# Forgetting attention's output projection: weight units in alternating order, more steps inside the last heads

## The reference, cut to what matters

```python
q, k, v, f_logit = jnp.split(x @ w_in, [D, 2 * D, 3 * D], axis=-1)
c = cumsum(log_sigmoid(f_logit + b_f))
s = q @ k.T * HEAD_DIM ** -0.5 + c[t] - c[s]     # per head, causal
o = softmax(s) @ v
return o @ w_o                                   # 1024 x 1024
```

## Time and profile before

| | us |
|---|---|
| median of three runs | 1881.05 |
| the profiled execution | 1880.14 |
| its span, first to last instruction | 1878.3 |
| PE busy | 1858.2 |
| DVE busy | 926.3 |
| ACT busy | 706.8 |

### The profile page before, as it was taken

The page is one execution under the profiler, slowest core; times in us unless marked ns, Lnnn a source line. Parts: engine busy times, 40 slices in busy tenths (PEclk is TensorE's granted clock), DMA queues, the critical chain, the costliest instruction groups (busy, mean ns, idle before and its releaser), DMA issues.

```text
span 1878.3 us, 24126 instructions
## 1 busy us (share of the span) xinstructions
PE 1858.2 (99%) x8779; PEld 1529.3 (81%) x8779; DVE 926.3 (49%) x1336; ACT 706.8 (38%) x1162; POOL 24.4 (1%) x44
## 2 busy tenths in 40 slices
PE   9999999999998999999999999999999999999998
PEld 7888888877776888888888888888888788888888
DVE  5444434356886544444344444434379644444332
ACT  5232223246775432323233232323267432322332
POOL 1000000000000000000000000000000000000000
PEclk9999999999999999999999999999999999999999
DMA  5223223331111332332333223223323223232332
GB/s 169 94 97 100 88 91 103 121 96 64 55 57 34 102 101 90 100 98 81 102 111 112 91 99 100 87 88 107 121 82 82 82 90 100 89 100 89 93 104 85
DMA packets 56521, 176.33 MB, mean 94 GB/s; under 512 B 6800, under 2 KB 9360, under 8 KB 56464
## 3 DMA queue, kind: packets, MB, share of 16 engines
q1 hardware_dynamic: 56320, 175.54, 29.3%
q10 hardware_dynamic: 144, 0.03, 0.0%
HBM read 171.48 MB, written 2.10 MB: 92 GB/s over the span
## 4 chain that ended last, share of the span: by engine, by line
PE 95%; DVE 2%; ACT 1%; issue 0%; DMA 0%; POOL 0%; DVEq 0%; SPq 0%; POOLq 0%; ACTq 0%
PE bank L454 91%; PE bank L800 1%; PE bank L812 1%; PE bank L910 0%; ACT scratch L1345 0%; DVE w_lo L1418 0%; ACT wide_hi L1295 0%; PE bank L480 0%; PE bank L517 0%; PE bank L523 0%; PE bank L514 0%; DVE wide_lo L1832 0%; DVE wmax L1816 0%; DMA scratch<-x_dram 0%; DVE wide_lo L1824 0%
## 5 line engine op out<-in xcount | busy, mean ns | idle before, releaser
L1418 DVE TENSOR_TENSOR w_lo<-raw,w_hi 128x1024 fp32r<-128x1024 f32 (+1 forms) x343 | 392.4, 1144 | 816.9 <-ACT w_hi L1017 815.6
L1017 ACT ACTIVATE w_hi<-raw 128x1024 fp32r<-128x1024 f32 (+1 forms) x343 | 341.3, 995 | 846.3 <-PE bank L454 843.9
L454 PE MATMUL bank<-u_hi,w_hi 128*128 128x512 f32 (+1 forms) x1592 | 630.2, 396 | 0.3 <-DVE w_lo L1418 0.3
L454 PE MATMUL bank<-u_hi,w_lo 128*128 128x512 f32 (+1 forms) x1592 | 620.2, 390 | 0.0
L454 PE MATMUL bank<-u_lo,w_hi 128*128 128x512 f32 (+1 forms) x1592 | 620.0, 389 | 0.0
L454 PEld LDWEIGHTS bank<-u_hi,w_lo 128*128 128x128 f32 (+1 forms) x1592 | 298.1, 187 | 63.6
L454 PEld LDWEIGHTS bank<-u_hi,w_hi 128*128 128x128 f32 (+1 forms) x1592 | 298.6, 188 | 61.0 <-issue 1.1
L454 PEld LDWEIGHTS bank<-u_lo,w_hi 128*128 128x128 f32 (+1 forms) x1592 | 298.6, 188 | 59.4 <-issue 1.0
L454 PE MATMUL bank<-wide_hi,w_hi 128*128 128x512 f32 (+1 forms) x816 | 316.1, 387 | 0.8 <-issue 0.5
L454 PE MATMUL bank<-wide_hi,w_lo 128*128 128x512 f32 (+1 forms) x816 | 314.7, 386 | 0.0
L454 PE MATMUL bank<-wide_lo,w_hi 128*128 128x512 f32 (+1 forms) x816 | 314.6, 386 | 0.0
(11 more groups left out here) (186 smaller groups left out, 1279.6 us busy)
## 6 DMA issues: line engine op xcount, KB each, us to landing
raw<-ffn_in_dram SPq DMA_DIRECT2D x175, 512.0 KB, 3.2
raw<-ffn_out_dram SPq DMA_DIRECT2D x128, 384.0 KB, 3.0
raw<-mix_w_dram SPq DMA_DIRECT2D x51, 512.0 KB, 3.3
y_dram<-raw SPq DMA_DIRECT2D x8, 256.0 KB, 2.7
wide_hi<-wide_hi SPq DMA_DIRECT2D x7, 256.0 KB, 2.8
scratch<-x_dram SPq DMA_DIRECT2D x2, 512.0 KB, 8.0
raw<-ffn_in_dram SPq DMA_DIRECT2D x2, 256.0 KB, 3.7
scratch<-x_dram SPq DMA_DIRECT2D x2, 256.0 KB, 4.0
```

Of the source, the lines that this page charges most:

```text
L454: mm = pe.matmul(out, a, b, start=first and k == 0, stop=last and k == n - 1)
L1017: act.activation(w_hi[:, slot, 0:cols], raw[:, (base + r) % RAW, 0:cols], ACT.Copy)\
L1418: dve.tensor_tensor(w_lo[:, s, 0:cols], raw[:, r, 0:cols], f32(w_hi[:, s, 0:cols]), ALU.subtract).then_inc(w_ready, 1)
```

## The change

The eight output units lie in memory in the order `WO_ORDER`, as pairs (m, k): the first four alternate between pair 0 and pair 1. Unit 26 is thus (1, 0) and unit 27 is (0, 1). The host puts the weights in that order. `fox_out_pairs` replaces `first_out_pairs` for this mixer (the sliding window keeps the old one): seven steps of pair 0 (units 25 and 27), then seven of pair 1 (26 and 28), then kb 7 of each. The first output step moves to the sixth filler place of t = 13, and t = 16 uses four places. On ACT and DVE the step that splits unit 27 moves from the end of t = 15 to the end of t = 14, and the two pairs' residuals come after the third and the fourth unit instead of the second and the fourth.

```diff
+WO_ORDER = ((0, 0), (1, 0), (0, 1), (1, 1), (2, 0), (2, 1), (3, 0), (3, 1))
...
-            def out_pair(n, m, ready, per_pair):
+            def out_pair(n, m, ready, per_pair, unit_of=lambda m, k: len(WO_KBS) * m + k):
...
-                    at = n + len(WO_KBS) * m + k
+                    at = n + unit_of(m, k)
...
+            def interleaved(m, k):
+                return WO_ORDER.index((m, k))
+
+            def fox_out_pairs(n):
+                pairs = [out_pair(n, m, o_ready, 2, interleaved) for m in range(2)]
+                pe.wait_ge(qk_scaled, 2 * PAIRS)
+                for _ in range(PAIRS - 1):
+                    next(pairs[0])
+                    yield
+                pe.wait_ge(expd, TB * HEADS)
+                for _ in range(PAIRS - 1):
+                    next(pairs[1])
+                    yield
+                for pair in pairs:
+                    for _ in pair:
+                        pass
...
-                    yield from first_out_pairs(n + 2 * PAIRS - 2, [0] * 7 + [1], (qk_scaled, 2 * PAIRS), o_ready, 2,
-                                               (expd, TB * HEADS))
+                    yield from fox_out_pairs(n + 2 * PAIRS - 2)
...
-                    allowed = {HEADS - 3: range(KB - AHEAD), HEADS - 2: (0, 3, 6), HEADS - 1: (0, 3, 6),
-                               HEADS: (0, 4)}.get(t, range(KB))
+                    allowed = {HEADS - 3: range(KB - AHEAD + 1), HEADS - 2: (0, 3, 6), HEADS - 1: (0, 3, 6),
+                               HEADS: (3, 4, 5, 6)}.get(t, range(KB))
...
-                        if r % len(kbs) == len(kbs) - 1:
-                            post_pair(nn, 4 * i, 2 * (r // len(kbs)))
+                        done = ends if ends is not None and type(i) is int and i == 0 else pair_ends
+                        if r in done:
+                            post_pair(nn, 4 * i, 2 * done.index(r))
...
-                    if j + 1 < PAIRS or t == HEADS - 1:
+                    if j + 1 < PAIRS or t == HEADS - 2:
                         step(n)
                         n += 1
-                out_stage(n - 1, nn + 1, WO_KBS, UNIT, first_split=True)
+                out_stage(n - 1, nn + 1, WO_KBS, UNIT, first_split=True, ends=(2, 3))
...
-    mix_w = np.concatenate([w_v[0:1], w_f, w_v[1:5], qk[0:2], w_v[5:], qk[2:], wo(a["fox_w_o"][0]),
+    mix_w = np.concatenate([w_v[0:1], w_f, w_v[1:5], qk[0:2], w_v[5:], qk[2:],
+                            wo(a["fox_w_o"][0])[[2 * m + k for m, k in WO_ORDER]],
                             kv, columns(swa[:, 0:D], PAIRS), wo(a["swa_w_o"][0])])
```

More of the change, by code:

```diff
@@ L1114, in ffn, with out_stage @@
                 out_stage(base + IN_BODIES * IN_UNITS, nn + 1, OUT_KBS, OUT_COLS, last)
-            def out_stage(base, nn, kbs, cols, last=False, first_split=False):
+            def out_stage(base, nn, kbs, cols, last=False, first_split=False, ends=None):
                 units = 2 * len(kbs)
+                pair_ends = (len(kbs) - 1, units - 1)
                 def body(i, count=units):
@@ L1545, in ffn, with out_stage @@
                 out_stage(base + IN_BODIES * IN_UNITS, nn + 1, OUT_KBS, 0.5, OUT_COLS, last)
-            def out_stage(base, nn, kbs, scale, cols, last=False, first_split=False):
+            def out_stage(base, nn, kbs, scale, cols, last=False, first_split=False, ends=None):
                 units = 2 * len(kbs)
+                pair_ends = (len(kbs) - 1, units - 1)
                 def body(i, count=units):
@@ L1561, in body @@
                                      cols if r + LOOK < units else UNIT)
-                        if r % len(kbs) == len(kbs) - 1:
-                            mp = r // len(kbs)
+                        done = ends if ends is not None and type(i) is int and i == 0 else pair_ends
+                        if r in done:
+                            mp = done.index(r)
                             dve.wait_ge(unit_used, base + units * i + r + 1)
@@ L1746, in fox @@
                                           ALU.subtract).then_inc(o_ready, 1)
-                    if j + 1 < PAIRS or t == HEADS - 1:
+                    if j + 1 < PAIRS or t == HEADS - 2:
                         step(n)
                         n += 1
-                out_stage(n - 1, nn + 1, WO_KBS, 1.0, UNIT, first_split=True)
+                out_stage(n - 1, nn + 1, WO_KBS, 1.0, UNIT, first_split=True, ends=(2, 3))
             def window_q_lo(j):
```

## The result

The changed kernel takes 1891.61 us (median of five runs, 1890.48 to 1892.96) against 1881.05 us: a ratio of 1.0057, 95% interval 1.0046 to 1.0069. That is 10.6 us slower; 5.8 were forecast, and the range ended at 1890.3.

What follows compares the result with a forecast made beforehand. TensorE was taken to bound the kernel, busy 1858.2 of 1878.3 us. The terms +1.05, +3.04, +1.88 and -0.13 sum to +5.84 us on the 1881.05 median: forecast 1886.9 us, range 1884.5 to 1890.3.

Steps and rivals of the forecast that it cites:

- A to E: Sum's parts: early step, t=13, +1.05; unit 27 wait, t=15, +3.04; t=16 steps +1.88; tail -0.13; residuals, loads 0 us.
- a rival with a chance of 0.22: Behind the new 3 us PE waits the clock falls, 1.6 us each: 1888.5 or 1890.1 us; chance 0.22.
- no unit wait was hidden: Rival: faster hand-over of unit 27 or 28 hides one 3.04 us wait: +2.8, 1883.9 us; chance 0.10.
- The weights stand ready: Rival: from t = 15, units 27 to 29 are split before PE needs them: -1.4 us, 1879.6 us; chance 0.08.

Runs made afterwards that it cites:

- The kernel whose clock holds: Changed kernel plus twelve extra PE matmuls, result unread, in each of the two 3.0 us waits: 1886.89 us, ratio 1.0030.
- the last two experiments: Changed kernel without its early step, units 27 and 28 split early outside the ring, two choices of step places in t = 15: 1877.83 and 1877.39 us.
- the last kernel: As the kernel with units 27 and 28 split early, but t = 15 takes places 3, 5, 6 instead of 0, 3, 6: 1877.39 us.
- the kernel ahead of the last: Changed kernel, units 27 and 28 split early outside the ring, no early step, t = 16 also taking its first place: 1877.83 us.
- the short wait alone: Kernel before, plus only a PE wait at t = 15's first step for two extra ACT copies: 1884.32 us, ratio 1.0019.
- the long wait: Kernel before, plus only a PE wait at t = 15's first step for four extra ACT copies: 1886.36 us, ratio 1.0033.
- with the second wait filled: Changed kernel plus twelve extra PE matmuls ahead of kb 4 of the second pair only: 1888.74 us, ratio 1.0041.

## Why the prediction was wrong

**Right:** the direction, and A to E. Every wait came where the order of the queues put it, and the parts are off by 0.3 us at most once the clock's share is taken out. Their errors nearly all have one sign, so the stretch without the clock is 1.0 us longer than forecast. The kernel whose clock holds takes 1886.89 us, and the forecast was 1886.9: a match to 0.01 us is luck.

**Wrong:** the step that took a wait of 3 us on PE to cost 3 us. The sum has no term for the clock; the runs showed one of 1.29 + 2.8 = 4.1 us. The forecast left the clock to a rival with a chance of 0.22, on the ground that "the longest single wait now, 1.30 us, left the clock at 1.00". (It is the longest from 570 to 604 us; at 1460.62 us PE waits 1.40 us for line 1824, at a clock of 1.00 too.) That carried nothing for waits more than twice as long. Early in the kernel the trace had shown a fall behind a stretch in which PE was busy for 1.69 of 3.20 us; the new waits leave it less to do than that, and the nearest row therefore spoke for a fall. The traces of the changed kernel and of the experiments show it behind idle times of 1.49, 2.00, 2.22, 2.41, 3.02 (twice), 3.07 and 3.32 us.

**Wrong in size as well:** the rival took each fall for 1.6 us, from one stretch of 3.2 us at 1.2 GHz. The first slowed 2.7 us of matmuls and cost 1.29; the second slowed 6.1 us and cost 2.8. Two falls at 1.6 gave 1890.1, and the measured time is 1.5 us above it: 4.1 - 3.2 = 0.9 is the size of the falls, and the rest the parts' small excesses. The range was built on that figure and so ended too low.

The other rivals: no unit wait was hidden in the changed kernel. "The weights stand ready" was right as a mechanism, as the last two experiments show, but not as a description of the change: with the splits queued behind outputs that PE makes last, they can't stand ready.

**Open:** what decides about a fall behind shorter waits. The same pair of about 0.46 and 1.14 us in t = 13 was followed by slow matmuls in the profile without the early step and in that of the last kernel, and not in those of the kernel before and of the kernel ahead of the last. The nine times with the short wait alone are four from 1882.2 to 1883.2 us, four from 1885.8 to 1886.2, and one between, as if the clock fell in some executions and held in others. The six with the long wait are three from 1885.1 to 1885.2 us, at a mean granted clock of 0.998, and three from 1887.5 to 1887.9 at 0.996 or 0.997, as if a fall lasted longer in the second three; the median of 1886.36 lies between the groups. Only one execution of each kernel has a trace, so neither is shown.

## What to carry to other kernels

Before moving matrix work forward, find the instruction on the other engines that hands it its operands, and see what stands ahead of it in that engine's queue: here the split stood behind an output that PE itself had yet to finish, and a step taken from behind a wait came to stand in a longer one. Price a PE wait like those here (1.5 to 3.3 us) at its length plus a stretch at half clock, here 1.3 to 2.8 us more for one fall. Where it can't be removed, idle matmuls are a repair (here 4.1 us); a place for the operand outside the ring is the better one.

## What the runs showed of the hardware that was not expected

The time at half clock behind a wait was not of one length: after two waits of the same 3.02 us in one trace it was 2.7 and 6.1 us of matmuls, costing 1.29 and 2.8, and with the second wait filled the first one, now 3.07 us, cost 2.7. So the cost of a fall isn't set by the wait. And an idle time of 1.49 us was enough for a fall in one place, while 1.41 us in another, and 1.30 us in the kernel before, left the clock at 1.00. Nor does the length decide alone: the pair of about 0.46 and 1.14 us in t = 13 was followed by a fall in two profiles and by none in others.
